# Four small tiles of softmax bookkeeping change their place in the state buffer

## The reference

```python
u = rms_norm(x, norm_g) @ w_in                       # v_c b_c c_c z_c q k v z_a gates
y_a = (b_c * conv(c_c * v_c, conv_w) * silu(z_c)) @ w_conv_out
m = maximum(max(scores), sink)                       # windowed attention
p = exp(scores - m); p = p / (sum(p) + exp(sink - m))
y_b = (p @ v * silu(z_a)) @ w_attn_out
x = x + (g_a * y_a + g_b * y_b) @ w_out

mix = fox_mixer(x, attn_w_in, attn_b_f, attn_w_out)  # full causal attention, softmax
x = layer_norm(ALPHA * x + mix, ...)
u, g = split(x @ w_up)
x = layer_norm(ALPHA * x + (gelu(conv(g)) * u) @ w_down, ...)
x = x + sigmoid(x @ ple_w_gate + ple_b_gate) * (p @ ple_w_proj)
```

## Time and profile before

| | |
|---|---|
| median of 3 runs | 2476.72 us |
| the profiled execution, its own time | 2476.72 us |
| its span, from first to last instruction | 2475.0 us |
| TensorE busy | 2440.3 us (99%) |
| weight loads busy (beside the matmuls) | 2013.9 us (81%) |
| VectorE / ScalarE / GpSimd busy | 1550.9 / 1088.5 / 1323.5 us |
| moved by DMA | 267.24 MB, 108 GB/s in the mean |

### The profile page before, as it was taken

How to read it: one execution, slowest core, us unless ns; L and a number is a source line. 1 busy time by engine, 2 the same in 40 slices (tenths; PEclk the granted TensorE clock), 3 DMA queues, 4 the chain that set the end, 5 groups by cost and what they waited for, 6 DMA issues and landing times. The chain is left out here.

```text
span 2475.0 us, 36098 instructions
## 1 busy us (share of the span) xinstructions
PE 2440.3 (99%) x11658; PEld 2013.9 (81%) x11658; DVE 1550.9 (63%) x2240; ACT 1088.5 (44%) x2010; POOL 1323.5 (53%) x1092
## 2 busy tenths in 40 slices
PE   8999999999999999999999999999999999999999
PEld 5888888888788878888888888877788888878877
DVE  6555552344777785435666666756678777777785
ACT  4332333301666661126777777832433333344441
POOL 3798887433455554432111111244279888666683
PEclk9999999999999999999999999999999999999999
DMA  3222223579210015321111111431133333387652
GB/s 112 90 75 67 70 68 113 180 267 331 77 34 25 26 35 187 132 99 60 43 43 43 43 43 43 138 109 52 47 111 115 123 119 110 140 281 217 190 182 80
DMA packets 126498, 267.24 MB, mean 108 GB/s; under 512 B 13872, under 2 KB 14000, under 8 KB 126400
## 3 DMA queue, kind: packets, MB, share of 16 engines
q1 hardware_dynamic: 84800, 157.85, 20.2%
q10 hardware_dynamic: 41600, 108.19, 12.2%
HBM read 198.02 MB, written 67.96 MB: 107 GB/s over the span
## 5 line engine op out<-in xcount | busy, mean ns | idle before, releaser
L639 POOL TENSOR_SCALAR whi<-raw 128x512 fp32r<-128x512 f32 x194 | 142.1, 732 | 783.9 <-PE bank L867 394.4
L641 POOL TENSOR_TENSOR wlo<-raw,whi 128x512 fp32r<-128x512 f32 x194 | 275.2, 1419 | 16.2
L804 PE MATMUL bank<-a_hi,whi 128*128 128x512 f32 x464 | 182.6, 394 | 1.5 <-issue 1.5
L804 PE MATMUL bank<-b_lo,whi 128*128 128x512 f32 x464 | 181.4, 391 | 0.0
L654 POOL TENSOR_TENSOR wlo<-a,whi 128x512 fp32r<-128x512 f32 x114 | 165.3, 1450 | 17.1 <-ACT whi L1687 16.9
L867 PE MATMUL bank<-b_hi,whi 128*128 128x512 f32 x384 | 156.4, 407 | 0.0
L867 PE MATMUL bank<-b_hi,wlo 128*128 128x512 f32 x384 | 150.7, 392 | 0.0
L867 PE MATMUL bank<-b_lo,whi 128*128 128x512 f32 x384 | 149.9, 390 | 0.0
L804 PE MATMUL bank<-b_hi,whi 128*128 128x512 f32 x336 | 131.7, 392 | 0.7 <-DVE b_lo L2300 0.4
L804 PE MATMUL bank<-a_hi,wlo 128*128 128x512 f32 x336 | 130.8, 389 | 0.0
L804 PE MATMUL bank<-a_lo,whi 128*128 128x512 f32 x336 | 130.8, 389 | 0.0
(11 more groups left out here) (710 smaller groups left out, 7618.6 us busy)
## 6 DMA issues: line engine op xcount, KB each, us to landing
raw<-in_w SPq DMA_DIRECT2D x206, 256.0 KB, 2.6
a<-in_pairs SPq DMA_DIRECT2D x152, 256.0 KB, 2.7
wd_scr<-wd SPq DMA_DIRECT2D x55, 256.0 KB, 5.0
wd<-in_down SPq DMA_DIRECT2D x44, 256.0 KB, 4.7
xs_scr<-made ACTq DMA_DIRECT2D x40, 256.0 KB, 2.6
fc<-c_scr ACTq DMA_DIRECT2D x16, 512.0 KB, 3.6
h_scr<-up_y ACTq DMA_DIRECT2D x13, 512.0 KB, 2.6
raw<-wd_scr SPq DMA_DIRECT2D x26, 256.0 KB, 2.8
```

The source lines that it names most:

```text
L639: nc.gpsimd.tensor_scalar(hi, src, 1.0, 1.0, ALU.mult, ALU.mult).then_inc(w_hi, 1)
L641: nc.gpsimd.tensor_tensor(lo, src, hi.bitcast(F32), ALU.subtract).then_inc(w_lo, 1)
L804: last = nc.tensor.matmul(psum_ap, ws[w][:, k, :], a[:, kt, hs(h)], start=(first and i == 0 and j == 0), stop=(final and i == n - 1 and j ...
```

## The change

The four lines that ask for `mx`, `neg_max`, `row_sum` and `sink_exp` move from ahead of `raw` to ahead of `row_inv`:

```diff
         total = 207 * 1024 + 512
 
-        mx = fixed("mx", [P, 8], F32)
-        neg_max = fixed("neg_max", [P, 8], F32)
-        row_sum = fixed("row_sum", [P, 8], F32)
-        sink_exp = fixed("sink_exp", [P, 8], F32)
         raw = [fixed(f"raw{b}", [P, HALF], F32) for b in range(2)]
         whi = [fixed(f"whi{s}", [P, KT, P], F32R) for s in range(2)]
         wlo = [fixed(f"wlo{s}", [P, KT, P], F32R) for s in range(2)]
...
         neg_sink = fixed("neg_sink", [P, 2 * NPAIR], F32)
+        mx = fixed("mx", [P, 8], F32)
+        neg_max = fixed("neg_max", [P, 8], F32)
+        row_sum = fixed("row_sum", [P, 8], F32)
+        sink_exp = fixed("sink_exp", [P, 8], F32)
         row_inv = fixed("row_inv", [P, 8], F32)
         a_hi_at = top[0]
```

## The result

The changed kernel takes 2508.16 us (median of 4 runs, 2506.12 to 2509.02), the kernel before 2476.62 us (median of 4 runs, 2476.30 to 2476.75): a ratio of 1.0124, 95% interval 1.0111 to 1.0136. The forecast was 2476.9 us with a range up to 2479.2 us. It missed by 31 us, and the sign was among the cases that had 0.05 together.

The account below looks back on a forecast made before the run. The prediction took TensorE's matmuls, one after the other, to bound the kernel. From 2476.72 us it added 0 for stationary operands, 0.2 for transfers and 0 for small tiles: 2476.9 us, range 2475.2 to 2479.2 us.

Parts of the forecast that it names:

- the cases that had 0.05 together: Slower outcomes past the 5.0 us bound: weight load 0.02, late transfers 0.02, something slower not named 0.01.
- What bounds the kernel: Whole kernel: TensorE, busy 2440.3 of 2475.0 us, sets the time; it costs its matmuls one after the other.
- Stationary operands: TensorE matmuls reading `whi` and `wlo` at their new addresses: 0 us taken, bounds 156 us gained and 645 us lost.
- The load outgrowing its matmul: Rival, matmuls reading `whi` or `wlo`: load grows over 38.7 ns, then 11.7 us per ns; 2488 to 3122 us; chance 0.02.
- the sign of being wrong that asked for another duration of the load together with another pitch: TensorE: a weight load other than 188 ns with the pitch moved from 226.7 ns would show the forecast wrong.
- the two signs that held: TensorE: 7.48 us for 33 matmuls of L1291 and 1789 matmuls in 405 us, if the forecast was right.
- The clash of the two reads: Rival, TensorE's stationary and moving rows: 128 B apart they stop meeting; 2321 us, or 2461 for a tenth; chance 0.03.
- Transfers into `raw`: 243 loads into `raw`: 0.1 us more each, nearly all covered; 0.2 us counted for two loads at the start.
- Small tiles: Maxima, negations, reciprocals and row-sum read-outs on the four small tiles: 0 taken, bound 4.0 us either way.
- 0.92 on no change: Whole kernel: chance given to the forecast of 2476.9 us together with its twin, no effect at all, 2476.7 us.

Follow-up runs that it names:

- e3_all_up: Kernel before with 128 B of padding in front of all tiles, so every tile moves up and distances stay: 2476.57 us, ratio 1.000.
- e1_raw_alone: Kernel before with only `raw` moved down by 128 B and the four small tiles put behind it: 2476.43 us against 2476.46, ratio 1.000.
- e15_one_slot: Kernel before with `raw` and slot 1 of `whi` and `wlo` moved down by 128 B, slot 0 left in place: 2492.80 us against 2476.24, ratio 1.0066.

## Why the prediction was wrong

**What bounds the kernel.** Right. TensorE sets the time, its waits hide nothing, and the loss is the growth of the pitch over the matmuls.

**Stationary operands, taken as 0.** This is the step that failed. The prediction said that "nothing of what a matmul costs follows from where its weights are", from `flip<-ct2hi,whi` and `bank<-ct1hi,cr0hi` with 389 ns each and equal pitches in two stages. The 389 ns are right (the 226.4 ns that the earlier trace rows gave for one stage is the count with the matmuls at the edges; by the starts it is 226.7 ns there too), and the inference isn't: in the kernel before all those tiles stand at multiples of 256 B from each other, so rows of that kernel compare two places and only one distance. They could not bear on a distance that the kernel does not have. The other support, tiles 32 B off the grid on ScalarE and VectorE, is of engines that show no second instruction reading beside the first, as TensorE shows a load beside a matmul. The prediction did state both bounds for this term, 645 us and -156 us, and then gave it no width at all in the range; 31.5 us lies well between them. What the runs showed in place of the 0: the pitch of matmuls with weights in `whi` or `wlo` goes from 226.7 to about 233 ns when those tiles stand 128 B off a multiple of 256 B from the moving tiles, and back to 226.7 ns when 128 B of padding restore it.

**The size.** In the stretch of L804 it is 233.3 - 226.7 = 6.6 ns a matmul, 3%. Over the whole kernel it is 31.5 us because the rest is spared: matmuls with weights in the large tiles keep their pitch, and the attentions lose only 1.2 and 2.2 us. There the matmuls of L867 stand in short groups between smaller ones, and the mean pitch inside these groups goes from 229.7 to 232.2 ns; why it grows less there is open.

**The rivals.** The load outgrowing its matmul had the right sign and the right place, with a wrong mechanism: loads kept 188 ns (so the sign of being wrong that asked for another duration of the load together with another pitch came true by half, and the two signs that held were the chain, 7.67 for 7.48 us, and the count, 1757 for 1789), and its reason, rows that straddle more pieces of 256 B, is theory A, refuted by `e3_all_up`. The clash of the two reads named the quantity that counts, the distance of the stationary and the moving rows, with the wrong sign. It asked what a clash in the kernel before would give back. The kernel before has nothing to give back that any run shows: its distances are of the kind that is free, no other distance was faster, and the change left it. The argument that a clash "would come and go with what lies beside it" speaks for the absence of a clash before, and says nothing on what a new distance brings.

**Transfers into `raw`.** The value of 0.1 us a load was too high: the median to landing of `raw<-in_w` is 2.6 us before and after, and `e1_raw_alone` gives 2476.43 against 2476.46 us, so no run shows the 0.2 us of the sum. The Trainium skill's rule on transactions of 256 B ("DMA: Bandwidth & Descriptors", "How a descriptor splits into AXI transactions") has no effect on the time here.

**Small tiles.** Right with 0. The changed kernel's rows of `neg_max` and `row_inv` (VectorE, as in the earlier trace rows) did not move:

```profile
L2508 DVE RECIPROCAL row_inv<-row_sum 128x1 f32<-128x1 f32 x128 | 20.7, 162 | 40.1 <-ACT fp L1560 39.9
L2503 DVE TENSOR_SCALAR neg_max<-mx 128x1 f32<-128x1 f32 x128 | 19.7, 154 | 4.4
```

**The chances.** 0.92 on no change rested on the fact that no instruction moved. A term that no row of the trace shows, on the engine that bounds the kernel, with a price of 11.7 us for each nanosecond, should have carried more.

## What to carry to other kernels

Where TensorE is bound by its matmuls and loads weights beside them, the distance in bytes between the stationary and the moving tile can be part of the schedule; here it had to be a multiple of 256 B. Round the large blocks of a layout up to that (one line of padding did it) before small tiles are shuffled, and compare the count of matmuls in a fixed stretch afterwards, since neither waits nor the duration of a load show the loss. A row of the trace supports a zero only if the trace holds a case that differs in the quantity that the change changes.

## What the runs showed of the hardware that was not expected

- What a matmul takes depends, in this kernel, on where its neighbour's weights are loaded from (232.5 and 235.0 ns instead of 226.5 at the handovers with 128 and 32 B). With the rows at a distance that is no multiple of 256 B the pitch of a 512-column fp32 matmul goes from 226.7 ns to between 228.9 ns (64 B, mean over L804) and 234.3 ns (160 B), at a granted clock of 1.00. The Trainium skill says of TensorE and ScalarE that they never wait on anyone in the buffer ("SBUF — State Buffer", "Who interferes with whom") and that loading the next weights takes no read bandwidth from the running matmul ("TensorE: Matmul & The Clock Gate", "Step-by-step: what each phase is for"). At free distances the trace agrees, with 226.7 ns; at the others TensorE's two reads are not free of each other by the handovers above, and the measurement decides. Against other engines the first of these statements stands here: GpSimd's writes in `e15_one_slot` left 226.7 ns.
- Where the tiles lie on their own does not matter: 128 B up for all of them is 2476.57 us, and whether transfers land on a multiple of 256 B makes no difference that can be measured, 2476.43 us.
- That the two reads clash over a shared part of the buffer is an explanation that would fit a loss of this kind, and it is not shown. What the part would be, how it would be divided within 256 B, why 64 B costs a third of what its neighbours do, and why the first load out of step is free at 64 and 192 B, no run here shows.
